# Causal mask inside the row maximum, and another order of ScalarE's work in the attention of a hybrid decoder layer

## What is computed

```python
sc = (einsum('bqhr,bkr->bhqk', q_lat, ckv) + einsum('bqhe,bke->bhqk', q_rope, k_rope)) * SOFTMAX_SCALE
sc = where(k_pos <= q_pos, sc, NEG_BIG)
p = softmax(sc, axis=-1)
...
h = exp(da_t) * h + einsum('bgjp,bgn->bgjpn', x_t * dt_t, b_t)      # sample tokens' states
y = einsum('bgjpn,bgn->bgjp', h, c_t)
...
out = x + rmsnorm(concat(o_attn, y_ssm) @ w_out)
```

## Time and profile before

| | us |
|---|---|
| median of 3 runs | 515.91 (514.53 to 517.11) |
| the profiled execution: time | 513.86 |
| its span, first to last instruction | 512.1 |
| PE busy | 497.9 |
| DVE busy | 352.1 |
| ACT busy | 289.2 |
| POOL busy | 78.6 |

### The profile page before, as it was taken

The page is one execution under the profiler, slowest core; times in us unless marked ns, Lnnn a source line. Parts: engine busy times, 40 slices in busy tenths (PEclk is TensorE's granted clock), DMA queues, the critical chain, the costliest instruction groups (busy, mean ns, idle before and its releaser), DMA issues.

```text
span 512.1 us, 12310 instructions
## 1 busy us (share of the span) xinstructions
PE 497.9 (97%) x4754; PEld 445.4 (87%) x4754; DVE 352.1 (69%) x756; ACT 289.2 (56%) x592; POOL 78.6 (15%) x100
## 2 busy tenths in 40 slices
PE   8999999999999999999999999999999999999992
PEld 7999999899999999999999875766666699999992
DVE  4843668695557675563542588699998899996643
ACT  6643312206347266462644796678986879664531
POOL 1321000000001010000000133244455301110520
PEclk9999999999999999999999999999999999999998
DMA  7642112239798888989997244966434677889712
GB/s 255 252 163 85 64 61 103 89 111 334 249 312 293 287 310 277 316 273 313 300 281 276 32 80 124 221 142 110 143 90 154 227 258 240 284 260 380 250 54 83
DMA packets 58076, 104.16 MB, mean 203 GB/s; under 512 B 7465, under 2 KB 27346, under 8 KB 57890
## 3 DMA queue, kind: packets, MB, share of 16 engines
q1 hardware_dynamic: 58018, 103.37, 63.1%
HBM read 95.68 MB, written 7.76 MB: 202 GB/s over the span
## 4 chain that ended last, share of the span: by engine, by line
PE 87%; DVE 4%; ACT 3%; DMA 3%; issue 1%; SPq 0%; ACTq 0%; DVEq 0%
PE pm L1673 20%; PE pm L1674 19%; PE pm L1675 19%; PE px L1769 4%; PE px L1789 3%; PE px L1955 3%; PE pm L1974 3%; PE pm L1942 2%; DMA dec<-ac_dram 2%; PE px L1891 1%; PE px L1918 1%; PE pm L1966 1%; PE pm L1921 1%; DMA xraw<-in_xT 1%; PE px L1957 1%
## 5 line engine op out<-in xcount | busy, mean ns | idle before, releaser
L1673 PE MATMUL pm<-xw_hi,w_lo 128*128 128x260 f32 x544 | 157.9, 290 | 1.0 <-DVE w_lo L1160 0.8
L1674 PE MATMUL pm<-xw_lo,w_hi 128*128 128x260 f32 x544 | 153.7, 283 | 0.0
L1675 PE MATMUL pm<-xw_hi,w_hi 128*128 128x260 f32 x544 | 153.6, 282 | 0.0
L601 ACT ACTIVATE w_hi<-w_raw 128x1024 fp32r<-128x1024 f32 (+1 forms) x70 | 72.5, 1038 | 82.0 <-PE pm L1675 70.1
L1014 DVE TENSOR_TENSOR w_lo<-w_raw,w_hi 128x1024 fp32r<-128x1024 f32 (+1 forms) x70 | 86.3, 1239 | 35.3 <-ACT w_hi L601 35.3
L1673 PEld LDWEIGHTS pm<-xw_hi,w_lo 128*128 128x128 f32 x544 | 102.4, 188 | 3.3 <-issue 1.2
L1674 PEld LDWEIGHTS pm<-xw_lo,w_hi 128*128 128x128 f32 x544 | 102.4, 188 | 0.2
L1675 PEld LDWEIGHTS pm<-xw_hi,w_hi 128*128 128x128 f32 x544 | 102.4, 188 | 0.0
L1673 PE MATMUL pm<-mix_hi,w_lo 128*128 128x260 f32 x224 | 63.8, 285 | 0.1
L1675 PE MATMUL pm<-mix_hi,w_hi 128*128 128x260 f32 x224 | 63.3, 283 | 0.0
L1673 PEld LDWEIGHTS pm<-mix_hi,w_lo 128*128 128x128 f32 x224 | 42.2, 188 | 0.6 <-DVE mixlo_a L1391 0.3
(11 more groups left out here) (297 smaller groups left out, 1090.7 us busy)
## 6 DMA issues: line engine op xcount, KB each, us to landing
page<-in_cache SPq DMA_DIRECT2D x128, 288.0 KB, 4.2
w_raw<-in_w_in SPq DMA_DIRECT2D x32, 512.0 KB, 5.3
w_raw<-in_w_out SPq DMA_DIRECT2D x32, 512.0 KB, 5.4
dec<-ac_dram SPq DMA_DIRECT2D x16, 256.0 KB, 9.7
hring<-in_ssm_state SPq DMA_DIRECT2D x8, 512.0 KB, 7.9
o_ssms<-hring SPq DMA_DIRECT2D x8, 512.0 KB, 6.7
w_raw<-in_w_qb SPq DMA_DIRECT2D x6, 384.0 KB, 2.8
xraw<-in_xT SPq DMA_DIRECT2D x8, 260.0 KB, 5.0
```

Source lines behind the costliest of these rows:

```text
L601: act.activation(w_hi[s][:, 0:n], w_raw[s][:, 0:n], ACT.Copy).then_inc(a_whi, 1)
L1673: pe.matmul(out, wl, xh, start=start, stop=False)
L1674: pe.matmul(out, wh, xl, start=False, stop=False)
L1675: return pe.matmul(out, wh, xh, start=False, stop=stop)
```

## The change

The mask leaves TensorE. A tile `causal` of 512 columns, zero except for the causal triangle in its last 128, is made by GpSimd before the middle stage. The row maximum becomes one operation that adds it to the score block, negates, writes the block back to its PSUM bank and takes the row minimum; the exponential then scales by -1. ScalarE's two roundings of `ident_r` and `mask_r` go. `orow` moves by 512 bytes to make room.

In ScalarE's loop `state_decay(s)` moves from the end of step s - 1 to behind the third exponential of step s; `copy_k(s + 2)` moves to behind `mix_high`, in front of squares, decays and the fourth exponential; `decays(5)` moves from before the loop into step 0. On VectorE the fourth row maximum and the third inverse come before the state update, `head(5)` follows `y_pair`, step 0's state update moves up to the same place, and `group_scale(1)` of step 6 moves behind the gating. TensorE's order is otherwise unchanged.

```diff
@@ -221,13 +220,14 @@
             CM_ = o
         if name == "qlp":
             dxs = at("dxs", [P, 2, 8, NB], F, o)
+            causal = at("causal", [P, NT], F, o + 512)
         if name == "ckbc":
             yt = at("yt", [P, NT], F, o)
             prod = at("prod", [P, 4, NS], F, o)
         if name == "olT":
             gacc = at("gacc", [P, NT], F, o)
         if name == "qrl":
-            orow = at("orow", [P, 2 * P], F, o)
+            orow = at("orow", [P, 2 * P], F, o + 512)
         if name == "qru":
             ys = at("ys", [P, 8, NB], F, o)
             gs = at("gs", [P, 8, NB], F, o + 256)
...
@@ -794,11 +791,6 @@
                 stack_high(1)
             if i == 22:
                 stack_high(6)
-            if i == 11:
-                act.wait_ge(s_const, 16)
-                act.activation(mask_r, cm[:, M_MQ, :], ACT.Copy).then_inc(a_mask, 1)
-                act.wait_ge(a_mask, 1)
-                act.activation(ident_r, cm[:, M_ID, :], ACT.Copy).then_inc(a_mask, 1)
             if i == 12:
                 act.wait_ge(v_dt, 4)
                 act.activation(dtw[:, 3, 0:64], dtw[:, 1, 0:64], ACT.Exp).then_inc(a_dt, 1)
...
@@ -855,7 +847,7 @@
             if h >= 2:
                 act.wait_ge(p_ring, RING_AT["t", h - 2, 3] + 1)
             i0, n, k = poff(b), P * (b + 1), 4 * (h % 2) + b
-            act.activation(pr[:, h % 2, i0:i0 + n], px[:, n_ % 3, 0:n], ACT.Exp, bias=nmx[:, k:k + 1], accum_out=rsum[:, k:k + 1])\
+            act.activation(pr[:, h % 2, i0:i0 + n], px[:, n_ % 3, 0:n], ACT.Exp, bias=nmx[:, k:k + 1], scale=-1.0, accum_out=rsum[:, k:k + 1])\
                .then_inc(a_p, 1)
 
         def copy_pt(h, b):
...
@@ -910,7 +902,6 @@
             exps(0, b)
         act.wait_ge(v_zs, 1)
         act.activation(mix_hi[:, 0:H, NT:TT], zs, ACT.Copy).then_inc(a_zh, 1)
-        decays(5)
         act.wait_ge(a_dx, 1)
 
         for s in range(H - 1):
...
@@ -918,20 +909,22 @@
             exps(s + 1, 1)
             copy_pt(s, 0)
             exps(s + 1, 2)
+            if s < 6:
+                state_decay(s)
             copy_pt(s, 1)
             if s:
                 mix_high(s - 1)
+            else:
+                decays(5)
+            if s + 2 < H:
+                copy_k(s + 2)
             if s in (1, 2):
                 gated_square(SQUARES[s][0])
             if s in FALLS:
                 decays(FALLS[s][0][0])
-            if s == 0:
-                state_decay(0)
             exps(s + 1, 3)
             if 3 <= s < 6:
                 gated_square(SQUARES[s][0])
-            if s + 2 < H:
-                copy_k(s + 2)
             copy_pt(s, 2)
             copy_pt(s, 3)
             if s == 6:
...
@@ -946,8 +939,6 @@
                     decays(h)
             if s in (1, 2):
                 gated_square(SQUARES[s][1])
-            for n in STATE_DECAYS.get(s, ()):
-                state_decay(n)
 
         copy_pt(H - 1, 0)
         copy_pt(H - 1, 1)
...
@@ -1368,10 +1359,12 @@
 
         def mask_max(h, b):
             n = 4 * h + b
-            x = px[:, n % 3, :]
+            x, w = px[:, n % 3, 0:P * (b + 1)], P * (b + 1)
+            if n == 0:
+                dve.wait_ge(g_mask, 2)
             dve.wait_ge(p_s, n + 1)
-            dve.tensor_reduce(nmx[:, 4 * (h % 2) + b:4 * (h % 2) + b + 1], x[:, 0:P * (b + 1)], AX.X, ALU.max,
-                              negate=True).then_inc(v_m, 1)
+            dve.tensor_tensor_reduce(x, x, causal[:, NT - w:NT], -1.0, -NEG, ALU.add, ALU.min,
+                                     nmx[:, 4 * (h % 2) + b:4 * (h % 2) + b + 1]).then_inc(v_m, 1)
 
         def inverse_sum(h, b):
             dve.wait_ge(a_p, 4 * h + b + 1)
...
@@ -1457,32 +1450,31 @@
             inverse_sum(s + 1, 0)
             mask_max(s + 1, 2)
             inverse_sum(s + 1, 1)
-            if 0 < s < 6:
-                state_update(s)
             if s == 6:
                 inverse_sum(s + 1, 2)
             mask_max(s + 1, 3)
+            if s < 6:
+                inverse_sum(s + 1, 2)
+                state_update(s)
             if s:
                 mix_low(s - 1)
             else:
                 dve.wait_ge(a_zh, 1)
                 dve.tensor_tensor(mixlo_a[:, 0:H, NT:TT], zs, mix_hi[:, 0:H, NT:TT].bitcast(F), ALU.subtract)
-                head(5)
-            if s < 6:
-                inverse_sum(s + 1, 2)
             if s in PAIRS:
                 y_pair(PAIRS[s][0])
+            if s == 0:
+                head(5)
             for h in MASKS[1].get(s, ()):
                 head(h)
             inverse_sum(s + 1, 3)
             if s == 6:
                 group_scale(0)
-                group_scale(1)
-            if s == 0:
-                state_update(s)
             if s < 6:
                 dots(s)
             gated(s)
+            if s == 6:
+                group_scale(1)
             if s == 1:
                 y_pair(PAIRS[s][1])
 
...
@@ -1585,6 +1577,9 @@
             pool.wait_ge(v_ev, UNIT0[XI[t]] + 2)
             pool.tensor_copy(xlast[:, t, :], xbc[:, t, NT - 3:TT]).then_inc(g_last, 1)
 
+        pool.wait_ge(p_sc, NSTEP)
+        pool.memset(causal[:, 0:NT - P], 0.0).then_inc(g_mask, 1)
+        pool.tensor_copy(causal[:, NT - P:NT], cm[:, M_MQ, :]).then_inc(g_mask, 1)
         for n in range(2 * NCH):
 
             c, g = n // 2, n % 2
...
@@ -1946,14 +1941,12 @@
             pe.wait_ge(a_ring, RING_AT["k", h] + 1)
             pe.wait_ge(v_qsl, STACK_AT[h])
             if h == 0:
-                pe.wait_ge(a_mask, 2)
                 pe.wait_ge(v_krl, 1)
             for b in blocks:
                 n, w = 4 * h + b, P * (b + 1)
                 if n >= 3:
                     pe.wait_ge(a_p, n - 2)
                 pe.matmul(px[:, n % 3, 0:w], q[:, h, P * b:P * b + P], kn[:, h % 2, 0:w], start=True, stop=False)
-                pe.matmul(px[:, n % 3, P * b:w], ident_r, mask_r, start=False, stop=False)
                 pe.matmul(px[:, n % 3, 0:w], qs[h][:, P * b:P * b + P], kr_lo[:, 0:w], start=False, stop=False)
                 pe.matmul(px[:, n % 3, 0:w], qs[h][:, P * b:P * b + P], kr_hi[:, 0:w], start=False, stop=True)\
                   .then_inc(p_s, 1)
```

More of the change, by code:

```diff
@@ L99 @@
 ADDS = {1: (1,), 2: (2,), 3: (3,), 4: (5,), 5: (6,), 6: (7,)}
-STATE_DECAYS = {0: (1,), 1: (2,), 2: (3,), 3: (4,), 4: (5,)}
 DOTTED, PAIRED = [0, 0, 4, 8, 8, 12, 16, 20], [2, 3, 5, 6, 7, 8]
@@ L250, in build @@
     nmh, alpha, rs, lsum, epsc, nmx, rsum = (small[k] for k in ("nmh", "alpha", "rs", "lsum", "epsc", "nmx", "rsum"))
-    ident_r = at("ident_r", [P, P], R, CM_ + 4 * P * M_MQ)
-    mask_r = at("mask_r", [P, P], R, CM_ + 4 * P * M_ML)
     def col(c):
@@ L283, in build @@
     s_hs0 = sem("early_states_stored")
-    a_mask, a_gf, a_out = sem("mask_rounded"), sem("group_factor_done"), sem("out_copied")
+    g_mask, a_gf, a_out = sem("mask_set"), sem("group_factor_done"), sem("out_copied")
     v_cb, a_fall = sem("cb_masked"), sem("decay_exponents_done")
```

## The result

The changed kernel took 524.88 us (median of 4 runs, 523.48 to 526.34) beside 515.31 of the kernel before on the same chip: a ratio of 1.0192, 95% interval 1.0169 to 1.0214. All ratios here are to runs of the kernel before on the same chip; one such run, of 1726.82 us, is left out as slow. On the 515.91 from which the prediction started that is 525.8: slower, as forecast, but nearly twice as much (+9.9 us against +5.7), and 0.8 above the range. The profiled execution took 523.48 (span 521.6), against 519.6 forecast for it.

A forecast was written before the change was run, and what follows sets the result against it. TensorE was taken as the bound. Stalls of 9.65 us, less 2.76 (masks), 0.91 (state decays) and 0.5 (fifth decays), plus 0.2 (tail), gave +5.7 us: 519.6 profiled, 521.6 as a median, range 518.0 to 525.0.

The forecast's parts named there:

- four waits: Steps 1 to 4, second half of `outs`: TensorE stalls 2.30 us each for ScalarE's third copy of probabilities.
- marks 2 to 4: Attention loop, starts of `outs(s, 0)` in steps 2 to 4: forecast 12.7 and 12.8 us apart.
- marks 1 to 2: Starts of `outs(s, 0)` in steps 1 and 2, with a second `y_pair` between: forecast 14.7 us apart.
- the tail's 0.2: VectorE's chain after the last scores: `group_scale(1)` behind the gating and accumulator reads lose 0.2 us (0 to 0.6).
- So nothing further is late, with 0.9 us in hand: After the late fourth exponential: normalised block and next head's first exponential still reach TensorE in time, 0.9 us spare.
- Step 0 has neither decays nor square there: 1.77, no stall: Step 0, ScalarE's queue behind the keys' copy: 1.77 us behind the mark, so TensorE does not stall.
- the decays' term: Loop start, moving decays 5: 0.5 us gained, top 1.2, bottom 0 should the early state decay wait for its load.
- the rival of the clock at 0.04: TensorE's clock falls in the new stalls: up to 8.6 us more per step, one such step 530.2; chance 0.04.
- the masks' 2.76: TensorE between the pre-loop and last scores: mask matmuls removed gain 6 x 0.46 = 2.76 us.
- the stalls of 0.42 and 0.49: Old kernel's steps 1 and 2: moving state decays off the first exponential's path gains 0.42 + 0.49 = 0.91 us.
- the fifth decays' 0.5: Loop start, head 1's first exponential: moving decays 5 from ahead of it, with masks removed, gains 0.5 us.
- Break-even: Attention loop: gains of 2.76 + 0.91 + 0.5 are cancelled by a stall of about 1.0 us a step.

The follow-up runs named there:

- filler: Changed kernel, TensorE repeating a product into the bank that the last transposes of steps 1 to 4 overwrite; ratio 1.0126 with two products, 1.0129 with one.
- half the filler: Changed kernel with one added product of 0.86 us ahead of the last transposes of steps 1 to 4; 521.21 us, ratio 1.0129.
- full filler: Changed kernel with two added products of 0.86 us each ahead of the last transposes of steps 1 to 4; 521.81 us, ratio 1.0126.
- split kernels: Kernel before with the mask alone changed and two of four state decays ahead of the second probability copy: 513.66 us; also decays 5 moved: 512.99 us.

## Why the prediction was right in kind and too small

**Right.** The bound (TensorE), the place (ScalarE's copy of the keys waits for the mark, five times, 7.5 us in all), the queue behind it in its order, four waits (2.13 for 2.30) and a small one in step 5 (0.32 for 0.45), marks 2 to 4 (12.88 and 12.69 for 12.7 and 12.8), marks 1 to 2 (14.81 for 14.7), the tail's 0.2 (10.83 from the last scores to the projection, 10.62 before), and no load of GpSimd's mask on the path. Row maximum: 0.70 for 512 columns as before, and 0.14 for reading the accumulator where 0.08 was taken.

The miss is 4.2 us, 9.9 for 5.7. Two steps of the prediction failed; the second is the larger.

**The step that failed first: "So nothing further is late, with 0.9 us in hand".** It was worked out for a step with the state already loaded and applied to step 0 without a look at it. "Step 0 has neither decays nor square there: 1.77, no stall" priced TensorE's second half of `outs` alone, though decays 5 and a state decay had been moved into the step, ahead of the copy. In step 0 VectorE comes to head 2's row maxima behind the state update, a `y_pair`, head 5, the last inverse sum, the dots and the gating. In the trace after the update met its load first:

```profile
333.80 1.14 DVE L1329 SCALAR_TENSOR_TENSOR hring<-bcs,dxs,hring 128x128 f32<-128x128 f32 x4 [2.50 <-DMA bcs<-bc_dram]
...
338.56 1.35 DVE L1337 CUSTOM_DVE_ANT_0 prod<-hring,bcs 128x128 f32<-128x128 f32 x1
...
340.44 0.28 DVE L1366 CUSTOM_DVE_ANT_0 px<-px,causal 128x128 f32<-128x128 f32 x1
```

The row maximum started at 340.44, with mark 0 at 334.09; TensorE waited 0.62 and 0.90 and step 0 took 12.49 where 10.5 was forecast. The prediction named the load only as a bottom of the decays' term (0 in place of 0.5). The long step has two causes, the load and the late fourth exponential, each enough alone: with the copy back, step 0 is 12.68; with the update back, 13.88; with update and state decay back, 12.85; with all three back, 10.97. The price is 1.5 us in the trace. By the ratios with the clock kept, 1.0126 to 1.0107, it is about 1.0 us, but their intervals overlap.

**The step that failed second: the rival of the clock at 0.04**, "and the busy work around each stall speaks against it". It doesn't: 10.6 us of work stand between two waits of 2.13, and the clock still fell. The sum left this term out. The rival's size was wrong too, the other way. It was taken as one step at half speed, up to 8.6 us; one fall costs 1.45 to 1.65, since the clock is back after some 3 us, but in the traces one to three of the four waits bring one. In the profiled execution it was one fall (1.6 us), in the runs 3.3 us (ratio 1.0192 against 1.0126 and 1.0129 with filler). Falls in a varying number may also widen the spread, 523.5 to 526.3 against 520.8 to 521.7 with half the filler, but that is not shown: the run of 523.59 had a lower granted clock (0.987) than that of 526.17 (0.990), and the full filler's runs spread over 2.0 us.

**The parts in ratios.** 5.5 (what was counted) + 1.0 (step 0) + 3.3 (clock) = 9.8, of 9.9 measured. These are differences along one row of kernels, so that they add up proves nothing; what tests the prediction is the 5.5 against its 5.7.

**Right for a reason that was not seen: the masks' 2.76.** The term holds only because the same change takes the state decays from ahead of the first exponential. Alone the masks give nothing that can be told (0.9989), as ScalarE was 0.14 us from the limit in the undisturbed steps and past it between marks 1 and 3 (the stalls of 0.42 and 0.49). The prediction booked masks and state decays as two gains that stand by themselves; that of the masks needs the other. What the state decays give without the masks was not tried.

**Partly luck: the fifth decays' 0.5.** Mark 0 came 0.3 us sooner in the profiled execution. The base was one trace with a wait of 0.38; the other traces with the old place waited up to 2.42, those with the new one 0.90. What the move is worth therefore depends on when the load lands, and the prediction did not see this.

**Break-even.** "About 1.0 us a step" of stall: the kernel with the copy back, whose waits in steps 1 to 4 are 0.33, 1.40, 0.32 and none above 0.3, came out even (1.0013): 2.3 us of waits and 2.2 us of loss in step 0, against the 4.0 that the prediction set as the total gain.

Left open: why the clock fell behind one wait of 2.13 us and not behind the next like it. The waits, the work between them and the neighbours' activity look alike in the windows; no run tells them apart. Why marks 3 to 5 of the split kernels stay 10.70 apart was read (the first exponential waits 0.37 for VectorE's row maximum) but not tried.

## What to carry to other kernels

When a waiting instruction is moved ahead of others in an in-order queue, price the queue behind it in every iteration by itself, the first above all: there the loads are still on their way, and moved work meets them. Before booking a gain on the engine that bounds, look at the slack of the engine that feeds it: 0.46 us a head less of TensorE was worth 0.14 until ScalarE's work ahead of the exponential moved. Give a wait of TensorE that comes back in every step the price of its clock too: with waits of 2.13 us here it was 3.3 us. A filler matmul into a bank about to be overwritten is a cheap test, and here it made the kernel 3 us faster. And read a wait for a load in more than one trace before pricing its removal.

## What the hardware showed unexpectedly

TensorE's granted clock fell to 0.50 behind waits of 2.13 us amid full work, in one to three of four steps and not in the same ones from kernel to kernel; none of the profiled runs with waits of 1.28 or 0.42 us in their place showed a fall in the loop. It fell behind the single wait of 2.41 with the mask alone as well, and behind that of 2.42 with the split, but not behind one of 2.12 at the same place in the kernel with the copy of the keys alone. The same load (`dec`) landed 9.76, 11.04 and 11.54 us after its issue in three kernels, and `bcs` and `hring` 12.7 to 12.9. The four dots of a head took 0.29 us each in one step and 0.27, 0.30, 0.69 and 1.35 in another, the slow ones beside a GpSimd operation; row maxima, with one operand in PSUM, kept their time (0.70 for 512 columns). The accumulator read behind the row maximum takes 0.14 us, that behind the dots 0.08.
